# Heads of four attention branches turned by VectorE blocks and GpSimd transfers instead of TensorE

## Chip, cores and metric

One NeuronCore of a Trainium2 chip runs the whole program. The metric is device time in microseconds, the median of several executions.

## What is computed

One layer of a decoder trunk on 256 tokens of width 4096: a normalisation, one projection into all the queries, keys and values of four parallel token mixers, the mixers, a gated merge with an output projection, and a retrieval feed-forward block. What matters here are the scores of the mixers, each a product of a query head with a key head of 128 features:

```python
def qk(t, n, gi):
    return apply_rope(rmsnorm(heads(t, n), qk_gain[gi]), cos, sin)
o_a = stick_breaking_attention(heads(a_q, 4), heads(a_k, 4), heads(a_v, 4))
o_b = dsa_attention(qk(b_q, 4, 0), qk(b_k, 1, 1), ...)
o_c = nsa_attention(qk(c_q, 4, 2), ..., qk(c_ks, 1, 4), ..., qk(c_kw, 1, 5), ...)
o_d = dilated_attention(qk(d_q, 6, 6), qk(d_k, 2, 7), ...)
# in each: s = einsum('bthd,bshd->bhts', q, k) * scale
```

The output has float32 precision. The large products are therefore made three times, on a high and a low part of each operand.

## The kernel before

The program is one stream of 704 slots. A slot is one 512 KB piece of weights (256 rows by 512 columns): SyncE loads it into one of four buffers `w_raw`, ScalarE copies it rounded into `w_hi` (`hi`, line 1207), VectorE forms the rest `w_lo` (`lo`, line 1616), and TensorE runs twelve products of 128x512 on it (`products`, lines 676, 679 and 683; `branch_products`, lines 724, 726 and 730). A conversion may run up to three slots ahead of TensorE, since `hi` of slot s waits for the products of slot s-4 (`chunk_used`). Everything else is put between the slots by hand: on each engine a function `between(s)` issues, after the slot's main work, what tables give for slot s. No scheduler moves anything, and each engine runs its list in order. So an operation of VectorE in slot s is issued some two to three slots ahead of TensorE's slot s.

Slots 0 to 175 are the input projection, in 11 groups of 16 slots. Each group is copied from the accumulators to `proj` (tokens on the partitions) by `evacuate_in` (line 1232), three slots after its end. `norm_piece` normalises and ropes the heads of b, c and d on VectorE, in eight pieces per branch, and raises `heads_ready`. Slots 176 to 287 are the merge stage: per block of 512 output columns one slot of gate products (its result goes through `gates` on ScalarE) and one or two slots of branch products, whose result `merge` on VectorE multiplies with the gate (line 1861), which empties the accumulator bank for the next block.

The scores need queries and keys with the features on the partitions. `turn(n)` (line 780) does this with TensorE: it transposes two heads for both halves of the tokens, four transposes of 128x128, into a bank of `side`, and ScalarE copies the bank to `feat` (`copy_turned`, line 1241) three slots later. The table `TURNS` gives slot, bank, branch and heads. The passes of the softmax branches start in the slots of `PASS_AT`: `scores` (line 854) in that slot, `mask_scores` on VectorE 3 slots later, `exponentials` on ScalarE 4, `turn_probs` on TensorE (line 865) 5, `normalise` on VectorE (lines 1786 to 1800) 6, `weigh_values` on TensorE 7. Pass 6 is the last but one of branch c. The stick-breaking branch a has its scores on line 899, in slots 189 and 205.

The merged rows are already turned later in the program without TensorE: `block_mix` (line 1883) transposes 32x32 blocks with VectorE, `mix_store` and `mix_load` on SyncE's queue write them to DRAM and read them back with the features on the partitions.

Of the kernel before, what the change touches and what calls it, by code (L numbers as in the profile page):

```python
# [28 lines left out]
P = 128  # L29
# [105 lines left out]
def source(s):  # L135

    pair = unrolled_pair(s)
    if pair is None:
# [38 lines left out]
PASS_AT = (75, 82, 110, 117, 124, 131, 138, 145, 157, 165)  # L177
# [56 lines left out]
def build(nc, io):  # L234
# [12 lines left out]
    def const(name, shape, dt=F32):  # L247
# [15 lines left out]
    feat = {"c": at("feat_c", [P, 6, S], F32, MG0), "b": at("feat_b", [P, 7, S], F32, MG0 + 8 * KB),  # L263
            "d": at("feat_d", [P, 8, S], F32, MG0 + 8 * KB), "a": at("feat_a", [P, 8, S], F32, XT0),
            "i": at("idx_t", [P, 3, S], F32, MG0 + 16 * KB)}
# [33 lines left out]
    cmp_zero = at("cmp_zero", [P, P], BF16, cursor[0] + 2 * 32 * 3 * NCMP * 2)  # L299
    dil = const("dil", [P, NT, 3, S])  # L300
# [137 lines left out]
    turned, turned_copied = sems("turned", "turned_copied")  # L438
    z_turned, z_hi_done, z_lo_done = sems("z_turned", "z_hi_done", "z_lo_done")
# [65 lines left out]
    def tile_rows(h):  # L505
        return slice(h * P, (h + 1) * P)

# [60 lines left out]
    with nc.Block() as block:  # L568
# [98 lines left out]
        def _(pe):  # L667
# [84 lines left out]
            def turn(n):  # L752

                s, b, br, blocks = TURNS[n]
                if br == "i":
                    pe.wait_ge(ident_loaded, 32)
                    evacuated(pe, 2)
                elif br == "a":
                    evacuated(pe, NG1 - 1)
                    pe.wait_ge(probs_copied, len(PASSES))  # L760
                    pe.wait_ge(out_lo_done, 6)
                else:
                    pe.wait_ge(heads_ready, "bcd".index(br) * NT + NT)
# [3 lines left out]
                if br == "c":  # L767
                    pe.wait_ge(cmp_ready, 1)
                    pe.wait_ge(out_lo_done, 2)
                for i, blk in enumerate(blocks):  # L770
                    for h in range(NT):
# [4 lines left out]
                        elif br == "i":  # L776
                            c, w = B_IQ + P * blk, P
                        else:
                            c, w = OUT_COL[br] + blk * HD if (br, blk) != ("b", 6) else B_VC, HD
# [3 lines left out]
            def turn_z():  # L783
                last = max(n for n, t in enumerate(TURNS) if t[0] < Z_TURN)
                pe.wait_ge(turned_copied, last + 1)
# [6 lines left out]
            def index_scores(h):  # L792
# [3 lines left out]
                q, nk = feat["i"], (h + 1) * P  # L796
# [6 lines left out]
            def cmp_hidden_part(q):  # L803

                if q == 0:
                    pe.wait_ge(zero_ready, 1)
                    pe.wait_ge(cmp_blocks, 1)
                    pe.wait_ge(turned_copied, 7)
# [25 lines left out]
            def scores(i):  # L834
# [5 lines left out]
                need = {"b": 7, "c": 10, "d": 14}[br]  # L840
                pe.wait_ge(turned_copied, need)
                f = feat[br]
                if br == "b":
                    pairs = [(r, f[:, 4, :]) for r in range(4)]
                elif br == "c":
                    pe.wait_ge(cmp_ready, 1)
                    key = (kt_cmp[:], f[:, 4, :], f[:, 5, :])[part]
                    pairs = [(r, key) for r in range(4)]
                else:
                    pe.wait_ge(z_lo_done, 1)  # L850
                    pairs = [(2 * g + s, f[:, 6 + s, :]) for s in range(2) for g in range(3)]
# [17 lines left out]
            def weigh_values(i):  # L869
                br, h, part = PASSES[i]  # L870
                pe.wait_ge(probs_copied, i + 1)
                if first_part(br, part):
# [3 lines left out]
                    if br == "c":  # L876
                        pe.wait_ge(turned_copied, 10)
# [15 lines left out]
            def stick_z_scores(u):  # L893
                pe.wait_ge(turned_copied, len(TURNS))
                if u:
                    pe.wait_ge(stick_arg, 1)
                for r in range(2):
# [1677 lines left out]
```

## Time and profile before

| | |
|---|---|
| median of 3 runs | 1907.03 us (1906.21 to 1907.64) |
| profiled execution | 1906.17 us |
| its span in the profile | 1904.1 us |
| granted TensorE clock | 1.000 of full |
| busy, TensorE / its weight loads | 1899.7 us / 1566.8 us |
| busy, VectorE / ScalarE / GpSimd | 1463.1 us / 986.2 us / 36.3 us |
| mean DMA traffic | 217 GB/s |

The profile is of one execution; its device time is 2.1 us longer than the span from the first to the last instruction. Times of the rows are microseconds from the span's start unless marked ns. A busy time on TensorE holds overlapping matmuls, so its rows are read by their starts.

### The profile page before, as it was taken

The page shows a single profiled execution, that of the slowest core. Times are in us where ns is not written, and L with a number is a line of the kernel's source. Part 1 is how long each engine was busy: PE and PEld are TensorE (multiplying, and loading weights), DVE is VectorE, ACT ScalarE, POOL GpSimd, SP SyncE. Part 2 cuts the span into 40 slices and gives each one's busy share as a digit, 9 for nine tenths or more (in the row PEclk, how much of TensorE's full clock was granted, in tenths as well). Part 3 has the DMA queues.
Part 4 walks back from the last instruction along what each step waited for, and adds up shares of the span by engine and source line. Part 5 has one row for each costly group of instructions (what it writes and reads, how often), then busy time and mean ns, then how long its engine had stood idle before and what let it go on. Part 6 is the DMA issues. An engine that isn't in the chain of part 4 may idle for free.

```text
span 1904.1 us, 25847 instructions
## 1 busy us (share of the span) xinstructions
PE 1899.7 (100%) x8941; PEld 1566.8 (82%) x8941; DVE 1463.1 (77%) x2139; ACT 986.2 (52%) x1214; POOL 36.3 (2%) x49
## 2 busy tenths in 40 slices
PE   9999999999999999999999999999999999999999
PEld 8888888888888888888888888888887788888887
DVE  6578775585556889989765555899988878999897
ACT  6654644444456655556454464444444455555553
POOL 0010010000000000000000000000000000000000
PEclk9999999999999999999999999999999999999999
DMA  9976667655655668877787776767766678666664
GB/s 321 353 223 166 167 177 202 172 157 157 190 178 175 186 189 289 271 235 233 258 252 239 216 226 218 233 209 214 222 204 194 198 205 290 222 215 222 217 221 155
DMA packets 198833, 412.69 MB, mean 217 GB/s; under 512 B 45793, under 2 KB 124257, under 8 KB 198081
## 3 DMA queue, kind: packets, MB, share of 16 engines
q1 hardware_dynamic: 174048, 369.35, 63.3%
q10 hardware_dynamic: 20976, 25.19, 3.9%
q0 software_dynamic: 3696, 16.65, 2.5%
q8 instruction: 71, 1.16, 0.2%
q14 instruction: 42, 0.34, 0.1%
HBM read 390.15 MB, written 20.97 MB: 216 GB/s over the span
## 4 chain that ended last, share of the span: by engine, by line
PE 99%; DMA 0%; SPq 0%; ACT 0%; DVE 0%; issue 0%
PE acc L676 25%; PE acc L679 25%; PE acc L683 25%; PE acc L724 3%; PE acc L726 3%; PE acc L730 3%; PE acc L1160 2%; PE side L1038 1%; PE side L1040 1%; PE side L1039 1%; PE acc L1166 1%; PE acc L1080 1%; PE acc L1085 1%; PE acc L1079 1%; PE side L854 1%; PE side L966 1%
## 5 line engine op out<-in xcount | busy, mean ns | idle before, releaser
L1616 DVE TENSOR_TENSOR w_lo<-w_raw,w_hi 128x1024 fp32r<-128x1024 f32 (+1 forms) x649 | 784.8, 1213 | 386.7 <-ACT w_hi L1207 381.9
L1207 ACT ACTIVATE w_hi<-w_raw 128x1024 fp32r<-128x1024 f32 (+1 forms) x649 | 681.0, 1052 | 690.6 <-PE acc L683 572.2
L676 PE MATMUL acc<-w_hi,xt_hi 128*128 128x512 f32 x1348 | 365.6, 393 | 0.0
L679 PE MATMUL acc<-w_hi,xt_lo 128*128 128x512 f32 x1348 | 360.7, 389 | 0.0
L683 PE MATMUL acc<-w_lo,xt_hi 128*128 128x512 f32 x1348 | 360.5, 389 | 0.0
L679 PEld LDWEIGHTS acc<-w_hi,xt_lo 128*128 128x128 f32 x1348 | 253.0, 188 | 53.3
L683 PEld LDWEIGHTS acc<-w_lo,xt_hi 128*128 128x128 f32 x1348 | 253.1, 188 | 53.0
L676 PEld LDWEIGHTS acc<-w_hi,xt_hi 128*128 128x128 f32 x1348 | 250.1, 188 | 51.5 <-issue 1.8
L676 PE MATMUL acc<-w_hi,x_hi 128*128 128x512 f32 x640 | 175.1, 395 | 0.0
L679 PE MATMUL acc<-w_hi,x_lo 128*128 128x512 f32 x640 | 171.5, 390 | 0.0
L683 PE MATMUL acc<-w_lo,x_hi 128*128 128x512 f32 x640 | 171.4, 390 | 0.0
L679 PEld LDWEIGHTS acc<-w_hi,x_lo 128*128 128x128 f32 x640 | 120.1, 188 | 25.7
L683 PEld LDWEIGHTS acc<-w_lo,x_hi 128*128 128x128 f32 x640 | 120.1, 188 | 25.6
L676 PEld LDWEIGHTS acc<-w_hi,x_hi 128*128 128x128 f32 x640 | 117.2, 188 | 22.2
L1560 ACT ACTIVATE t_hi<-t_raw 128x1024 fp32r<-128x1024 f32 x46 | 47.7, 1058 | 24.6 <-PE acc L1040 14.9
L2285 DVE TENSOR_TENSOR t_lo<-t_raw,t_hi 128x1024 fp32r<-128x1024 f32 x46 | 54.1, 1218 | 0.0
L1349 ACT ACTIVATE gate<-acc 128x512 f32<-128x512 f32 x64 | 34.8, 596 | 37.3 <-PE acc L683 37.3
L676 PE MATMUL acc<-w_hi,zt_hi 128*128 128x512 f32 x128 | 34.5, 391 | 0.0
L683 PE MATMUL acc<-w_lo,zt_hi 128*128 128x512 f32 x128 | 34.2, 389 | 0.0
L679 PE MATMUL acc<-w_hi,zt_lo 128*128 128x512 f32 x128 | 34.2, 389 | 0.0
L2271 DVE TENSOR_TENSOR t_raw<-w_raw 128x1024 f32<-128x1024 f32 x23 | 28.1, 1221 | 3.9 <-DMA w_raw<-in_stream 3.5
L1861 DVE TENSOR_TENSOR gate<-acc,gate 128x512 f32<-128x512 f32 x48 | 30.7, 681 | 0.0
(376 smaller groups left out, 2050.2 us busy)
## 6 DMA issues: line engine op xcount, KB each, us to landing
w_raw<-in_stream SPq DMA_DIRECT2D x504, 512.0 KB, 4.2
w_raw<-in_w_in SPq DMA_DIRECT2D x16, 496.0 KB, 4.0
w_raw<-in_w_in SPq DMA_DIRECT2D x16, 480.0 KB, 4.1
w_raw<-in_w_in SPq DMA_DIRECT2D x16, 464.0 KB, 3.8
w_raw<-in_w_in SPq DMA_DIRECT2D x16, 448.0 KB, 3.9
w_raw<-in_w_in SPq DMA_DIRECT2D x16, 432.0 KB, 3.8
w_raw<-in_w_in SPq DMA_DIRECT2D x16, 416.0 KB, 4.1
w_raw<-in_w_in SPq DMA_DIRECT2D x16, 400.0 KB, 3.8
```

Of the source, the lines that this page charges most:

```text
L676: pe.matmul(o[h], lhs(k0 + j, h)[0], wh[j], start=first and j == 0, stop=False)
L679: pe.matmul(o[h], lhs(k0 + j, h)[1], wh[j], start=False, stop=False)
L683: mm = pe.matmul(o[h], lhs(k0 + j, h)[0], wl[j], start=False, stop=last and j == 1)
L724: pe.matmul(o, lhs(k0 + j, h)[0], wh[j], start=first and j == 0, stop=False)
L726: pe.matmul(o, lhs(k0 + j, h)[1], wh[j], start=False, stop=False)
L730: mm = pe.matmul(o, lhs(k0 + j, h)[0], wl[j], start=False, stop=last and j == 1)
L1160: pe.matmul(o, xt(2 * kp + j, h)[p], w[0][j], start=kp == 1 and h == 1 and p == 0 and j == 0, stop=False)
L1207: nc.scalar.activation(w_hi[:, slot, 0:width], w_raw[:, slot, 0:width], ACT.Copy).then_inc(hi_ready, 1)
L1349: e = nc.scalar.activation(gate[:, n % 2, h, :], acc[:, 1, h, :], ACT.Sigmoid)
L1560: nc.scalar.activation(flat(hi_tile[:, d]), flat(raw[:, d]), ACT.Copy).then_inc(t_hi_done, 1)
L1616: nc.vector.tensor_tensor(w_lo[:, slot, 0:width], w_raw[:, slot, 0:width], w_hi[:, slot, 0:width].bitcast(F32), ALU.subtract).then_inc(lo_ ...
L2285: nc.vector.tensor_tensor(flat(lo_tile[:, d]), flat(raw[:, d]), flat(hi_tile[:, d]).bitcast(F32), ALU.subtract).then_inc(t_lo_done, 1)
```

## The change

The transposes on TensorE of b's heads 0 to 4 and of all heads of c, d and a go, with ScalarE's copies behind them. In their place, for each branch of the new table `BLOCKED` (slot, heads, parts):

- ScalarE copies the heads in slot s from `proj` into `head_rows`, ordered for the blocks (`copy_heads`);
- VectorE transposes 32x32 blocks in slot s+1 (`block_heads`, one instruction per part) into `head_blk`, with the token as the outer index and (head, half) as the inner one;
- GpSimd writes the four groups of 32 partitions to DRAM in four transfers per part and loads them back in one (`move_heads`).

The tiles `feat` are now [feature, token, head, half]. The score matmuls on TensorE read them directly through `head_tokens` and `head_all`, so from one token to the next they step over all heads and both halves of the tile: 40 B in b (5 heads), 48 B in c (6), 32 B in d (2 tiles of 4) and 64 B in a (8). The passes of c and d start four and three slots later. Blocks 5 and 6 of b and the index heads are still turned by TensorE.

```diff
 TURNS = [(52, 0, "i", (0,)), (53, 1, "i", (1,)), (54, 2, "i", (2,)),
-         (61, 2, "b", (5, 6)), (62, 3, "b", (0, 1)), (64, 2, "b", (2, 3)), (65, 3, "b", (4,)),
-         (104, 3, "c", (0, 1)), (106, 2, "c", (2, 3)), (107, 3, "c", (4, 5)),
-         (144, 2, "d", (0, 1)), (146, 2, "d", (2, 3)), (148, 2, "d", (4, 5)), (150, 2, "d", (6, 7)),
-         (182, 0, "a", (0, 1)), (183, 1, "a", (2, 3)), (184, 2, "a", (4, 5)), (185, 3, "a", (6, 7))]
+         (61, 2, "b", (5, 6))]
+BLOCKED = {"b": (60, 5, 1), "c": (107, 6, 1), "d": (147, 8, 2), "a": (180, 8, 1)}
...
-PASS_AT = (75, 82, 110, 117, 124, 131, 138, 145, 157, 165)
+PASS_AT = (75, 82, 114, 121, 128, 135, 142, 149, 160, 168)
...
+        feat[b] = [at(f"feat_{b}{i}", [P, P, heads // parts, NT], F32, to + i * heads // parts * KB) for i in range(parts)]
+        head_rows[b] = at("head_rows_" + b, [P, parts, 4, heads // parts, NT, 32], F32, to)
...
+    def head_tokens(br, q, h):
+        return head_all(br, q, h, h + 1)[:, 0]
+    def head_all(br, q, h0=0, h1=NT):
+        n = BLOCKED[br][1] // BLOCKED[br][2]
+        return feat[br][q // n][:, :, q % n, h0:h1].rearrange("p t h -> p h t")
...
             def scores(i):
...
-                pe.wait_ge(turned_copied, need)
-                f = feat[br]
+                pe.wait_ge(head_moved, heads_moved(br))
...
-                    mm = pe.matmul(side[:, r // 2, (r % 2) * S:(r % 2) * S + nk], f[:, q, tile_rows(h)],
-                                   key[:, 0:nk], start=True, stop=True)
+                    keys = kt_cmp[:] if key is None else head_all(br, key, 0, h + 1)
+                    mm = pe.matmul(side[:, r // 2, (r % 2) * S:(r % 2) * S + nk], head_tokens(br, q, h),
+                                   keys, start=True, stop=True)
...
             def evacuate_in(g):
+                if g == 9:
+                    act.wait_ge(head_stored, 64 * head_parts("d"))
...
+            def copy_heads(br):
+                _, heads, parts = BLOCKED[br]
+                n = heads // parts
+                if br == "a":
+                    evacuated(act, NG1 - 1)
+                    act.wait_ge(chunk_used, CH_MIX)
+                else:
+                    act.wait_ge(heads_ready, "bcd".index(br) * NT + NT)
...
+                for i in range(parts):
+                    for h in range(NT):
+                        c0 = OUT_COL[br] + i * n * HD
+                        e = nc.scalar.activation(head_rows[br][:, i, :, :, h, :].rearrange("p b k j -> p k b j"),
+                                                 proj[:, h, c0:c0 + n * HD].rearrange("p (k b j) -> p k b j", b=4, j=32),
+                                                 ACT.Copy)
+                    e.then_inc(head_copied, 1)
...
+            def block_heads(br):
+                parts = BLOCKED[br][2]
+                for i in range(parts):
+                    dve.wait_ge(head_copied, head_parts(br) - parts + i + 1)
+                    if br == "c":
+                        dve.wait_ge(scores_ready, 2)
+                    nc.vector.transpose(head_blk[br][i][:].rearrange("p b (t x) -> p b x t", t=32),
+                                        head_rows[br][:, i].rearrange("p b k h j -> p b (k h) j"))\
+                        .then_inc(head_blocked, 1)
...
+            def move_heads(br):
+                parts = BLOCKED[br][2]
+                if head_parts(br) > parts:
+                    pool.wait_ge(head_moved, heads_moved(br) - 16 * parts)
+                for i in range(parts):
+                    pool.wait_ge(head_blocked, head_parts(br) - parts + i + 1)
+                    for a in range(4):
+                        pool.dma_start(head_d[br][:, :, a, i].rearrange("b j x -> j b x"),
+                                       head_blk[br][i][32 * a:32 * a + 32]).then_inc(head_stored, 16)
+                pool.wait_ge(head_stored, 64 * head_parts(br))
+                for i in range(parts):
+                    pool.dma_start(feat[br][i][:].rearrange("p (a t) k h -> p a (t k h)", a=4),
+                                   head_d[br][:, :, :, i].rearrange("b j a x -> (b j) a x")).then_inc(head_moved, 16)
...
             branch_rstd("b")
+            move_heads("b")
             branch_rstd("c")
...
+            move_heads("c")
             branch_rstd("d")
+            move_heads("d")
...
             pool.dma_start(tri[:], io["tri"]).then_inc(stick_loaded, 16)
+            move_heads("a")
```

VectorE's list around pass 6 of branch c, before the change, from the mask of that pass (slot 141) to its normalising multiply (slot 144); `proj` and `rope_tmp` are d's heads being roped, `probs` the probabilities:

```order
L1769 SCALAR_TENSOR_TENSOR probs_62<-side,causal 128x1024
L1772 TENSOR_REDUCE small<-probs_62 128x4
L1774 TENSOR_SCALAR small<-small 128x4
L1616 TENSOR_TENSOR w_lo<-w_raw,w_hi 128x1024
L1661 TENSOR_TENSOR proj<-proj,rope 128x1024
L1662 TENSOR_TENSOR proj<-proj,rope_tmp 128x1024
L1616 TENSOR_TENSOR w_lo<-w_raw,w_hi 128x1024 x2
L1656 TENSOR_TENSOR rope_tmp<-proj,rope 128x8x64
L1657 TENSOR_TENSOR rope_tmp<-proj,rope 128x8x64
L1786 TENSOR_SCALAR small<-small 128x4
L1787 RECIPROCAL small<-small 128x4
L1791 TENSOR_TENSOR small<-small 128x4
```

The same pass in the changed kernel, slots 145 to 148, where the rope pieces are the last of branch d:

```order
L1829 SCALAR_TENSOR_TENSOR probs_68<-side,causal 128x1024
L1832 TENSOR_REDUCE small<-probs_68 128x4
L1834 TENSOR_SCALAR small<-small 128x4
L1663 TENSOR_TENSOR w_lo<-w_raw,w_hi 128x1024
L1708 TENSOR_TENSOR proj<-proj,rope 128x1024
L1709 TENSOR_TENSOR proj<-proj,rope_tmp 128x1024
L1663 TENSOR_TENSOR w_lo<-w_raw,w_hi 128x1024 x2
L1745 STREAM_TRANSPOSE head_blk_d_100<-head_rows_d 128x4x8x32
L1745 STREAM_TRANSPOSE head_blk_d_101<-head_rows_d 128x4x8x32
L1846 TENSOR_SCALAR small<-small 128x4
L1847 RECIPROCAL small<-small 128x4
L1851 TENSOR_TENSOR small<-small 128x4
```

Two block transposes stand ahead of the normalisation, where two rope operations of half a piece stood.

VectorE's list at the start of the merge stage before the change, from the end of branch d's output to the first merges (the first `rows<-acc,gate` belongs to slot 181):

```order
L1807 TENSOR_TENSOR ot_d_lo<-side,ot_d_hi 128x256
L1616 TENSOR_TENSOR w_lo<-w_raw,w_hi 128x1024 x5
L1861 TENSOR_TENSOR rows<-acc,gate 128x512 x2
L1616 TENSOR_TENSOR w_lo<-w_raw,w_hi 128x1024 x3
L1861 TENSOR_TENSOR rows<-acc,gate 128x512 x2
```

And in the changed kernel:

```order
L1867 TENSOR_TENSOR ot_d_lo<-side,ot_d_hi 128x256
L1663 TENSOR_TENSOR w_lo<-w_raw,w_hi 128x1024 x2
L1745 STREAM_TRANSPOSE head_blk_a<-head_rows_a 128x4x16x32
L1921 TENSOR_TENSOR rows<-acc,gate 128x512 x2
L1663 TENSOR_TENSOR w_lo<-w_raw,w_hi 128x1024 x3
```

The transpose of branch a stands directly ahead of the first merge, and d's last output is three slots nearer to it.

## Rows read from the trace of the kernel before

**Rows 1.** The page: busy times, and the chain that ended last by engine
```profile
PE 1899.7 (100%) x8941; PEld 1566.8 (82%) x8941; DVE 1463.1 (77%) x2139; ACT 986.2 (52%) x1214; POOL 36.3 (2%) x49
...
PE 99%; DMA 0%; SPq 0%; ACT 0%; DVE 0%; issue 0%
```

**Rows 2.** TensorE's timeline around one turn: start, length, engine, line, operation, count
```profile
434.80 1.08 PE L683 MATMUL acc<-w_lo,xt_hi 128*128 128x512 f32 x4
435.71 0.60 PE L780 MATMUL side<-ident,proj 128*128 128x128 f32 x4
...
437.07 1.08 PE L679 MATMUL acc<-w_hi,xt_lo 128*128 128x512 f32 x4
437.99 1.07 PE L683 MATMUL acc<-w_lo,xt_hi 128*128 128x512 f32 x4
...
439.80 1.07 PE L679 MATMUL acc<-w_hi,xt_lo 128*128 128x512 f32 x4
```

**Rows 3.** Line 780: count, shortest, median and longest ns, first and last start
```profile
L780 PE MATMUL side<-ident,proj x64: 270/272/273, 137.1 to 547.4; 128*128 128x128 f32 x62, 128*64 128x128 f32 x2
```

**Rows 4.** ScalarE's groups from 100 to 720 us: count, busy us, mean ns, idle before
```profile
L1207 ACT ACTIVATE w_hi<-w_raw 128x1024 fp32r<-128x1024 f32 x207 | 218.2, 1058 | 156.0 <-PE acc L683 122.5 <-PE acc L730 31.2 <-DMA w_raw<-in_w_in 1.8
...
L1277 ACT ACTIVATE cmp_pc<-cmp_in 128x512 bf16<-128x512 f32 x13 | 8.0, 617 | 3.3 <-DVE cmp_in L1714 3.3
```

**Rows 5.** VectorE's groups from 100 to 720 us
```profile
L1696 DVE TENSOR_TENSOR cmp_b<-feat_b,pe_t 128x240 f32<-128x240 f32 x4 | 2.0, 576 | 0.0
...
L1675 DVE TENSOR_TENSOR idx_sum<-idx_sum,idx_tmp 128x256 f32<-128x256 f32 x3 | 1.3, 425 | 0.1
...
L1883 DVE STREAM_TRANSPOSE mix_blk<-mix_rows 128x1024 f32<-128x1024 f32 x1 | 1.2, 1239 | 0.0
```

**Rows 6.** Timeline of all engines from 403 to 419.5 us, pass 6
```profile
404.14 1.22 DVE L1769 SCALAR_TENSOR_TENSOR probs<-side,causal 128x1024 f32<-128x1024 f32 x1 [2.46 <-PE side L854]
...
408.84 2.00 ACT L1207 ACTIVATE w_hi<-w_raw 128x1024 fp32r<-128x1024 f32 x2
...
410.38 2.36 DVE L1616 TENSOR_TENSOR w_lo<-w_raw,w_hi 128x1024 fp32r<-128x1024 f32 x2
...
414.59 1.23 DVE L1800 TENSOR_TENSOR probs<-probs,small 128x1024 f32<-128x1024 f32 x1
...
417.59 1.04 PE L865 MATMUL side<-ident,probs 128*128 128x128 f32 x8
```

**Rows 7.** Timeline from 518 to 534 us, start of the merge stage
```profile
519.62 1.25 ACT L1232 ACTIVATE proj<-acc,small 128x512 f32<-128x512 f32 x2
...
523.15 2.05 ACT L1207 ACTIVATE w_hi<-w_raw 128x1024 fp32r<-128x1024 f32 x2
...
526.52 1.28 DVE L1861 TENSOR_TENSOR rows<-acc,gate 128x512 f32<-128x512 f32 x2
...
529.32 0.62 PE L724 MATMUL acc<-w_hi,ot_b_hi 128*128 128x512 f32 x2
```

**Rows 8.** DMA issues (KB each, median us to landing), and GpSimd's first transfers in its timeline
```profile
mix_blocks<-mix_blk SPq DMA_DIRECT2D x32, 128.0 KB, 4.5
mix_t<-mix_blocks SPq DMA_DIRECT2D x8, 512.0 KB, 6.0
...
518.87 1.34 POOL L2456 DMA_DIRECT2D strict<-in_strict  x2 [137.05 <-PE acc L683]
```

**Rows 9.** TensorE's timeline around d's second score pass, six matmuls of 256 columns
```profile
486.23 1.07 PE L683 MATMUL acc<-w_lo,xt_hi 128*128 128x512 f32 x4
487.14 2.75 PE L854 MATMUL side<-feat_d 128*128 128x256 f32 x12
...
490.66 1.08 PE L679 MATMUL acc<-w_hi,xt_lo 128*128 128x512 f32 x4
```

More of the change, by code:

```diff
@@ L299, in build @@
     cmp_zero = at("cmp_zero", [P, P], BF16, cursor[0] + 2 * 32 * 3 * NCMP * 2)
+    head_blk = {"b": [at("head_blk_b", [P, 4, 5 * 64], F32, cursor[0])],
+                "c": [at("head_blk_c", [P, 4, 6 * 64], F32, MG0 + 8 * KB)],
+                "d": [at(f"head_blk_d{i}", [P, 4, 4 * 64], F32, PJ0 + i * row + in_cols(9).start * 4) for i in range(2)],
+                "a": [at("head_blk_a", [P, 4, 8 * 64], F32, XT0 + 40 * KB)]}
+    head_d = {b: nc.dram_tensor("head_blocks_" + b, (4, 32, 4, parts, heads // parts * 64), F32, kind="Internal").ap()
+              for b, (_, heads, parts) in BLOCKED.items()}
     dil = const("dil", [P, NT, 3, S])
@@ L506, in tile_rows, with heads_moved, head_parts @@
         return slice(h * P, (h + 1) * P)
+    def heads_moved(br):
+        return 16 * head_parts(br)
+    def head_parts(br):
+        return sum(BLOCKED[b][2] for b in list(BLOCKED)[:list(BLOCKED).index(br) + 1])
+    def head_tokens(br, q, h):
[3 more added lines that the diff above has]
+        return feat[br][q // n][:, :, q % n, h0:h1].rearrange("p t h -> p h t")
     def flat(ap):
@@ L757, in turn @@
                     evacuated(pe, 2)
[L758 to L761, printed above, removed]
                 else:
-                    pe.wait_ge(heads_ready, "bcd".index(br) * NT + NT)
+                    pe.wait_ge(heads_ready, NT)
                 before = [m for m in range(n) if TURNS[m][1] == b]
@@ L783, in turn_z @@
             def turn_z():
-                last = max(n for n, t in enumerate(TURNS) if t[0] < Z_TURN)
-                pe.wait_ge(turned_copied, last + 1)
+                pe.wait_ge(cmp_ready, 1)
+                evacuated(pe, (Z_COL + 2 * P - FIRST - 1) // 512 + 1)
                 for h in range(NT):
@@ L1240, in copy_turned @@
                     act.wait_ge(cmp_split, 8)
[L1241 removed]
+                first = blocks[0] - (5 if br == "b" else 0)
+                nc.scalar.activation(flat(whole[br][:, first:first + len(blocks), :]), side[:, b, 0:len(blocks) * S],
                                      ACT.Copy).then_inc(turned_copied, 1)
+            def copy_heads(br):
[4 more added lines that the diff above has]
+                    act.wait_ge(chunk_used, CH_MIX)
+                else:
+                    act.wait_ge(heads_ready, "bcd".index(br) * NT + NT)
+                if br == "b":
+                    act.wait_ge(cmp_split, 8)
+                if br == "c":
+                    act.wait_ge(cmp_ready, 1)
+                if br == "d":
+                    act.wait_ge(head_moved, heads_moved("c"))
+                for i in range(parts):
[5 more added lines that the diff above has]
+                    e.then_inc(head_copied, 1)
             def z_hi():
@@ L1485, in between @@
                         copy_turned(n)
+                for br, (at_slot, _, _) in BLOCKED.items():
+                    if s == at_slot:
+                        copy_heads(br)
                 if s == Z_TURN + LEAD:
```

43 lines of the change are left out of this document (23 added, 20 removed).

## Prediction

> **What bounds the kernel now.** I read the page first: TensorE is busy for the whole span and 99% of the chain that ended last is its own, so the time is the length of TensorE's instruction stream [rows 1]. Anything taken out of that stream is gained one for one, and anything that makes TensorE wait is lost one for one. Then the timeline of TensorE around one removed turn. From the start of the last four products of a slot (434.80) to the start of the second four of the next slot (437.07) pass 2.27 us with a turn between; one slot later the same stretch takes 1.81 us (437.99 to 439.80). A turn of four transposes so costs 0.46 us, 0.115 us each [rows 2]. The matmul durations of 272 ns [rows 3] overlap and must not be added up. Last, the timelines of VectorE and ScalarE where the change queues new work, to see how much room is left before TensorE needs what stands behind it.
>
> The sum is made against the profiled execution, 1906.2 us (span 1904.1), which is 0.9 us under the median of the runs, 1907.0; the result is then given against the median. About 0.2% (3.8 us) is what a measurement of this kernel can tell from no change.
>
> **Removed from TensorE.** Of 66 transposes on line 780 (64 are in the trace [rows 3]) the change keeps twelve, those of the index heads and of blocks 5 and 6 of b. Gone are 10 of b, 12 of c, 16 of d and 16 of a: 54 x 0.115 = **-6.2 us**, all of it on the path. The 14 ScalarE copies out of PSUM that followed them go too; in their place come ten copies from SBUF of 512 to 1024 columns, 0.62 us per 512 and 1.06 us per 1024 [rows 4]. That is about as much time as before, on an engine that is half idle: nothing by itself.
>
> **Added to VectorE.** Five block transposes: 1280, 1536, 2 x 1024 and 2048 columns. The one that the trace shows, 1024 columns into a packed tile, took 1.24 us [rows 5], which is 1.04 ns a column after 0.16 us of start. The new ones write each column 32 to 64 B from the last. No row shows such a write. The nearest row is a strided read: line 1696 takes its input 64 B apart, 240 columns in 576 ns, where 256 packed ones take 425 ns [rows 5]. After the same start that is 1.74 ns a column. So 2048 columns take between 2.3 and 3.7 us, 1024 between 1.24 and 1.94. VectorE has room in general; two places matter.
>
> *Slot 147/148, branch d.* In pass 6 TensorE turns probabilities five slots after the scores, and VectorE must have normalised them. Before, the scores ended at about 404.1, the normalising multiply started at 414.59 and was over 1.9 us before TensorE's turn at 417.59 [rows 6]. The pass moves by four slots, so I lay the same times over it. VectorE's last rope piece ends as its next w_lo starts, at 410.38. ScalarE is through its exponentials and one conversion at 409.84; in the same slot it empties group 8 (two copies, 1.25 us as for the last group [rows 7]: 411.1), then come the four new copies (some 0.55 us from start to start, a little under the row's 0.62: 413.3), and only then the next w_hi (414.3). VectorE's w_lo behind it ends at 415.5, the two block transposes take 2.3 to 3.9 us, and the three small operations (0.62 us) and the multiply (1.14 us) stand behind them: 419.6 to 421.1. TensorE waits **2.0 to 3.5 us**.
>
> *Slot 180/181, branch a.* In the merge stage TensorE's first product of slot 180 (529.32 before) needs the bank that VectorE's merge of block 0 empties. Before, that merge began at 526.52 [rows 7]. Now ScalarE, free at 523.15, does a w_hi (524.2), the two copies of 1024 (526.3) and the next w_hi (527.3); VectorE's w_lo ends at 528.5, the transpose of 2048 columns at 530.8 to 532.2, and the first half of the merge at 531.4 to 532.9. TensorE waits **2.1 to 3.6 us**.
>
> I take the middle of both, 2.8 + 2.8 = **+5.6 us**, since the write is like the packed row in kind and like the strided row in its steps. At b (slot 60/61) VectorE's queue has no TensorE consumer within five slots, and at c (107/108) no pass is open: nothing there.
>
> **Added to GpSimd.** Per part four stores and one load. The same pattern on other queues took 4.5 us to land for a store and 6.0 us for a load, and GpSimd issued two transfers in 1.34 us [rows 8]: 4 x 0.67 + 4.5 + 0.67 + 6.0 = 14 us. The tightest consumer is c, blocked in slot 108 and needed in slot 114: six slots of 2.72 us and the lead of some two that VectorE has, 21 us. a has eight slots, d twelve, b fourteen. Hidden, with 7 us to spare at the tightest. If that is used up, TensorE waits for the rest.
>
> **Moved into TensorE's operands.** The features now lie with the token outermost, so 60 score matmuls read query and key in steps of 40 B (b), 48 B (c), 32 B (d) and 64 B (a). The moving columns are 1536, 3072, 2304 and 1536, together 8448. Packed, six matmuls of 256 columns lengthened the same stretch from 1.81 to 4.43 us [rows 9], so 1.71 ns a column, in two passes of 0.85 ns. No row shows TensorE reading with such a step. Lower bound: nothing, if its port does not care. Upper bound: each read takes the 1.74 ns that VectorE needed [rows 5], twice a column, +1.77 ns x 8448 = 15.0 us. That row has the 64 B step of branch a; I take it whole for a (2.7 us) and half for the smaller steps of the others (6912 x 0.89 = 6.1 us): **+8.8 us**.
>
> The page "Advanced Engine Details and Errata" of the Trainium skill, section "SBUF Cachelines", speaks against this layout: SBUF is read in lines of 16 bytes, and full speed wants at least two hits on a line. It gives no price; by it every one of the four steps would pay in full, and the sum would end near 1923. VectorE's row at 64 B agrees with it; for TensorE nothing here shows it.
>
> **Sum.** -6.2 + 5.6 + 8.8 = +8.2 us: 1914.4 for the profiled execution, **1915 us** against the median.
>
> **Rivals.**
>
> 1. *The strides are free to TensorE.* For it: TensorE takes an fp32 column in 0.85 ns a pass and the products' columns in half of that, so it may fetch well ahead. Against it: the one strided row of the trace. Then only the two waits are left, -6.2 + 4.1 to 7.1, that is 1905 to 1908: no change.
> 2. *Strides free and the waits absorbed* (the other side). The waits rest on 2 to 3.5 us past the need at two places; if ScalarE's copies run before heads_ready costs anything, or TensorE's sequencer finds bank and probabilities in time, the removed transposes stand alone: 1907.0 - 6.2 = 1901. It decides where VectorE's transposes end over 2 us earlier than I lay them out. For it: before the change TensorE waited nowhere. It becomes faster by over 0.2% as soon as waits and strides cost together less than 2.4 us.
> 3. *Every strided read pays in full*, with the slow writes: -6.2 + 7.1 + 15.0 = +15.9, 1923.
> 4. *A transfer lands late*, in c first: each 1 us beyond the 7 us of room is 1 us of TensorE. With 5 us late and free strides: 1911.
>
> **How the numbers follow.** My forecast and rival 3 are one mechanism of two sizes: together 0.50 (0.36 and 0.14). Rival 1 has 0.34, rival 2 0.12, rival 4 0.04. Faster 0.12, same 0.36 (rival 1 and the smallest of the forecast's), slower 0.52. The range has to hold rival 1 and nearly all of rival 3 and leaves out rival 2: 1902 to 1924. The forecast's own range is 1911 to 1924.
>
> **What the changed profile would show.** Step 1: line 780's successor with 12 transposes, and 54 fewer matmuls. Step 2: in TensorE's waits one of 2 to 3.5 us for VectorE's probs at the turn of pass 6, and one for VectorE's rows in the first merge; a busy share of TensorE a little under 100%. Step 3: the 12 records of a d pass of 256 columns take clearly more than 2.6 us of the stream, and so do a's; if they take 2.6, rival 1 or 2 holds. Step 4: GpSimd's loads land before slots 75, 114, 160 and 189, with no TensorE wait for a feature tile. The block transposes' mean (1.24 or 1.94 us for 1024 columns) tells which end the waits take. I am wrong if TensorE's scores keep their length, or if it waits for something not named here, a transfer above all.

## The result, and the profile after

| | before | after |
|---|---|---|
| median of 4 runs each, us | 1906.99 (1906.21 to 1907.64) | 1929.04 (1927.91 to 1929.31) |
| ratio, 95% interval | | 1.0115 (1.0097 to 1.0132) |
| profiled execution, us (span) | 1906.2 (1904.1) | 1929.3 (1927.5) |
| mean granted TensorE clock | 1.000 | 0.997 |

The kernel became slower by 22 us. I had forecast 1915, with a range of 1902 to 1924: the sign was right, the size was wrong, and the time lies outside the range. Two single executions of the experiments, one of e5 at 5576 us and one of the kernel before at 7792 us, are left out.

The page of the changed kernel, busy times and chain, against [rows 1]:

```profile
PE 1916.7 (99%) x8887; PEld 1578.6 (82%) x8887; DVE 1475.7 (77%) x2144; ACT 986.3 (51%) x1210; POOL 50.6 (3%) x74
...
PE 98%; ACT 1%; DVE 1%; DMA 0%; issue 0%; SPq 0%; ACTq 0%
```

TensorE has 54 matmuls fewer (8941 to 8887), as counted, and is busy 17 us longer. The chain of the end now passes through ScalarE and VectorE for one per cent each; before it was TensorE's alone. So there are two things to look for: matmuls that take longer, and waits.

**The waits.** TensorE's waits after the change, what it waited for, us in total, times, longest:

```profile
PE side L882 <- DVE probs L1860: 3.3, 1, 3.3
PE acc L750 <- DVE rows L1921: 3.1, 1, 3.1
```

These are the two waits of the prediction, at the two places named. The timeline round the first, pass 6 with d's block transposes in front of its normalisation, which answers to [rows 6]:

```profile
429.57 2.19 ACT L1283 ACTIVATE head_rows_d<-proj 128x512 f32<-128x512 f32 x4
...
433.88 4.00 DVE L1745 STREAM_TRANSPOSE head_blk_d<-head_rows_d 128x1024 f32<-128x1024 f32 x2
...
438.35 1.23 DVE L1860 TENSOR_TENSOR probs<-probs,small 128x1024 f32<-128x1024 f32 x1
...
439.64 1.97 PE L882 MATMUL side<-ident,probs 128*128 128x128 f32 x8 [3.27 <-DVE probs L1860]
...
441.26 1.80 PE L702 MATMUL acc<-w_hi,xt_hi 128*128 128x512 f32 x4
...
442.89 1.08 PE L705 MATMUL acc<-w_hi,xt_lo 128*128 128x512 f32 x4
```

And round the second, a's block transpose in front of the first merge, which answers to [rows 7]:

```profile
540.65 2.01 ACT L1283 ACTIVATE head_rows_a<-proj 128x1024 f32<-128x1024 f32 x2
...
544.77 3.66 DVE L1745 STREAM_TRANSPOSE head_blk_a<-head_rows_a 128x2048 f32<-128x2048 f32 x1
...
548.29 1.25 DVE L1921 TENSOR_TENSOR rows<-acc,gate 128x512 f32<-128x512 f32 x2
...
549.10 1.19 PE L750 MATMUL acc<-w_hi,ot_b_hi 128*128 128x512 f32 x2 [3.11 <-DVE rows L1921]
550.09 1.06 PE L752 MATMUL acc<-w_hi,ot_b_lo 128*128 128x512 f32 x2
```

Read the chain backwards in each: TensorE starts as VectorE's last operation delivers, that operation starts as the transposes end, and those could not start until ScalarE's copies were done and a w_lo had been made. The transposes took 3657 ns for 2048 columns and 2.0 to 2.15 us for 1024, at the slow end of what I had bounded from [rows 5] (3.7 and 1.94 us) or a little beyond it.

**The clock.** In the last two fences something else is odd. Eight transposes take 1.97 us where the same eight took 1.04 [rows 6], and two products of the merge 1.19 and 1.06 where they took 0.62 [rows 7]. The busy times by stretch of 2 us (PE, PEld, DVE, ACT, POOL, then the granted TensorE clock, DMA share and GB/s) show why:

```profile
438.00:440.00 2.00, 0.36 (x2) 0.37 (x3) 1.93 (x4) 0.00 (x0) 2.00 (x5) 0.80 0.86 213
440.00:442.00 2.00, 2.00 (x10) 1.90 (x9) 1.85 (x2) 0.36 (x1) 1.05 (x2) 0.50 0.81 240
...
549.00:551.00 2.00, 1.90 (x5) 1.56 (x6) 1.85 (x3) 0.00 (x0) 1.98 (x4) 0.50 0.46 100
...
553.00:555.00 2.00, 2.00 (x6) 1.55 (x5) 0.00 (x0) 0.35 (x1) 0.00 (x0) 0.50 1.01 260
555.00:557.00 2.00, 2.00 (x9) 1.60 (x9) 1.25 (x2) 0.71 (x1) 0.54 (x1) 0.94 1.00 365
```

The number behind POOL's is the granted clock: 0.50 is the lower of the two levels, 1.2 GHz against 2.4. TensorE stood still ahead of both stretches, and came back at half speed. At the first place it got its full clock back after some 3 us, at the second after 6. The prediction had no term for this.

**The score matmuls.** TensorE's timeline round d's second score pass, six matmuls of 256 columns in two passes of fp32 each, which answers to [rows 9]:

```profile
507.82 1.08 PE L709 MATMUL acc<-w_lo,xt_hi 128*128 128x512 f32 x4
508.73 2.01 PE L871 MATMUL side<-feat_d,feat_d 128*128 128x256 f32 x4
...
513.84 1.52 PE L702 MATMUL acc<-w_hi,xt_hi 128*128 128x512 f32 x4
515.20 1.08 PE L705 MATMUL acc<-w_hi,xt_lo 128*128 128x512 f32 x4
```

From 507.82 to 515.20 pass 7.38 us; the same stretch took 4.43. The weight loads grew too. Load times of two tiles, least, median and longest ns:

```profile
L871 PEld LDWEIGHTS side<-feat_c x32: 341/343/373, 325.5 to 421.7; 128*128 128x128 f32 x32
...
L871 PEld LDWEIGHTS side<-feat_d x8: 312/324/337, 484.1 to 513.3; 128*128 128x128 f32 x8
```

against this one before the change:

```profile
L854 PEld LDWEIGHTS side<-feat_c x32: 186/190/192, 314.3 to 403.5; 128*128 128x128 f32 x32
```

Measured like this (from the start of the last product ahead of a pass to the start of the second group of products behind it), the twelve score passes take:

| pass (step in the change) | before | after | e1, both packed | e2, weights strided | e3, moving strided |
|---|---|---|---|---|---|
| b, 128 and 256 columns (40 B) | 2.72, 4.42 | 3.73, 6.33 | 2.72, 4.41 | 3.56, 4.50 | 3.66, 6.31 |
| c, 128 twice (48 B) | 2.72, 3.58 | 3.95, 4.77 | 2.72, 3.59 | 3.86, 4.68 | 3.64, 4.50 |
| c, 15 twice (queries 48 B, keys packed) | 3.58, 4.44 | 4.68, 5.54 | 3.58, 4.44 | 4.67, 5.54 | 3.59, 4.45 |
| c, 256 twice (48 B) | 4.81, 5.28 | 6.80, 7.15 | 4.80, 5.28 | 5.32, 5.64 | 6.64, 7.13 |
| d, 128 and 256 (32 B) | 3.17, 4.43 | 4.67, 7.38 | 3.16, 4.43 | 4.57, 4.68 | 4.62, 7.37 |
| a, 256 twice (64 B) | 2.23, 2.70 | 3.51, 3.99 | 2.23, 2.69 | 2.58, 3.03 | 3.51, 3.97 |
| sum | 44.1 | 62.5 | 44.1 | 52.6 | 59.4 |

(The last three columns belong to the experiments below.) The passes account for 62.5 - 44.1 = 18.4 us. The transposes' -6.2, the waits' 3.27 + 3.11 = 6.4 and what the stretches behind the waits lost besides close the span's +23.4 us. That last part: 435.30 to 442.89 is 7.59 us, where a run without the wait (e11 below) has 2.72, so 4.87 are lost, 1.6 more than the wait; in the merge stage the same comparison gives 12.63 against 6.35, that is 6.28, 3.2 more than the wait. The sum is -6.2 + 18.4 + 6.4 + 4.8 = 23.4. Its first term is the forecast's; e5 below measures -6.5.

**GpSimd's transfers** (KB each, median us from issue to landing) against [rows 8]:

```profile
head_blocks_c<-head_blk_c POOLq DMA_DIRECT2D x4, 192.0 KB, 4.2
feat_c<-head_blocks_c POOLq DMA_DIRECT2D x1, 768.0 KB, 7.9
```

c's stores were issued from 304.62, its load at 312.44, so it landed at 320.3, and TensorE's first pass on it began at 325.77. No TensorE wait names a feature tile. The transfers are hidden, as forecast, though with less room: from the first store to the landing pass 15.7 us where I had 14, and 5.4 us were left where I had 7.

### The profile page after: what moved, and what is told of

The parts are those of the page before. It is cut to its first block, busy times and chain, and to the rows that moved or that the text cites. A ratio compares the mean times of both kernels' runs of the same rounds, so it can differ in the third digit from the quotient of the medians.

```text
span 1927.5 us, 25751 instructions
## 1 busy us (share of the span) xinstructions
PE 1916.7 (99%) x8887; PEld 1578.6 (82%) x8887; DVE 1475.7 (77%) x2144; ACT 986.3 (51%) x1210; POOL 50.6 (3%) x74
## 4 chain that ended last, share of the span: by engine, by line
PE 98%; ACT 1%; DVE 1%; DMA 0%; issue 0%; SPq 0%; ACTq 0%
PE acc L702 25%; PE acc L705 25%; PE acc L709 25%; PE acc L750 3%; PE acc L752 3%; PE acc L756 3%; PE acc L1178 2%; PE side L871 2%; PE side L1056 1%; PE side L1057 1%; PE side L1058 1%; PE acc L1184 1%; PE acc L1098 1%; PE acc L1097 1%; PE acc L1103 1%; PE side L984 1%
## 5 line engine op out<-in xcount | busy, mean ns | idle before, releaser
L1335 ACT ACTIVATE probs<-probs,small 128x128 f32<-128x128 f32 (+2 forms) x44 | 18.3, 417 | 39.0 <-DVE small L1834 39.0
```

## The experiments

Twelve kernels ran, four to ten executions each; the kernel before, run beside each of them on the same chip, had medians of 1906.0 to 1906.8 us. The theory after the result: the removed transposes gain 6 us, the strided operands cost 18, the two waits 6.4, and the clock behind them some 4 more. The rivals: that the strides cost less and something else in the new route slows TensorE (GpSimd's transfers or VectorE's transposes beside it), and that the fall of the clock has a cause of its own.

### e1, e2, e3: which operand pays

Both operands, or one of them, are read with step 1 from the same tiles; nothing else changes. Here `packed` takes as many columns as are needed from the head's own stretch of 256 in the flattened tile. They are not the head's columns, so the scores of e1, e2, e3 and e5 are not the right ones; the amount of work is the same.

```diff
-                    keys = kt_cmp[:] if key is None else head_all(br, key, 0, h + 1)
-                    mm = pe.matmul(..., head_tokens(br, q, h), keys, ...)
+                    keys = kt_cmp[:] if key is None else packed(br, key, (h + 1) * P)
+                    mm = pe.matmul(..., packed(br, q, P), keys, ...)
```

e1 has both lines and the same two in a's scores, e2 the keys' alone, e3 the queries' alone.

> The changed kernel, but the score matmuls read both operands from the same feature tiles with a step of one element; the scores are then of the wrong columns. Everything else stays: copies, block transposes, transfers, slots. Theory 1 (the steps cost TensorE's reads): the stretches around the twelve groups of score matmuls fall back to their lengths of before, 18.4 us in sum, so 1910 to 1911 us; both waits of 3.1 to 3.3 us and the low clock behind them stay. Rival (the stretches are longer for another reason, such as tiles that a transfer has just written, or GpSimd's traffic): no change, 1929 us.

> As the changed kernel, but only the moving operand (the keys; in a the queries) is read with a step of one; the weights are still read with their steps, and the scores are of wrong columns. A pass of 15 columns took 0.24 us with strided weights, so the strided weight load itself takes that long. If a pass takes the longer of its load and its columns, the 128-column passes stay at 0.24 us and only the 44 passes of 256 columns get shorter, from 0.455 to 0.24 us: 9.5 us less, 1919 to 1920 us. If load and columns add up, the gain is 8448 columns x 2 x 0.94 ns = 15.9 us: 1913 us. If only the moving side pays (rival), all 18.4 us: 1911 us.

> The mirror: weights read with a step of one, the moving operand with its steps, scores of wrong columns. If a pass takes the longer of load and columns, only the 16 passes of 15 columns and the 128-column passes of branch c gain, some 2.2 + 0.5 us: 1926 us. If load and columns add up, or the weight loads are what pays (rival), it falls by more than 5 us, to below 1924 us.

Measured: e1 1908.63 us (1906.35 to 1910.54), e2 1916.41 (1914.68 to 1917.36), e3 1924.81 (1924.46 to 1925.25). The table above has their passes. In e1 every pass is back at its length of before to 0.01 us, with the new engines' work and the transfers still running beside it: only the steps lengthened the passes. In e2 the weights alone make 8.5 us of it, in e3 the moving operand alone 15.3, together 18.4 and not their sum, 23.8. In each pass it is about the longer of the two that counts: the greater of e2 and e3, added up over the twelve, is 17.9. Where 256 columns move, the moving operand sets the length; where 15 move, the weights do; at 128 both are about equal. Weight loads run beside the matmul before them, and a late one shows only where the matmul is short.

In its passes e2 gave back 62.5 - 52.6 = 9.9 us, the 9.5 of its first expectation (the longer of load and columns): beside 256 columns the slow weight loads are mostly hidden (0.1 to 0.5 us a pass). Its time came out 3 us under that expectation's 1919 to 1920. In its profiled run the stretches round the two waits are shorter than in the changed kernel as well, 6.90 us against 7.59 and 11.32 against 12.63, though the waits are as long (3.28 and 3.08): 2.0 us less time lost to the clock. e3 is the same case: 3.1 us from the passes where 2.7 were expected, and 1.4 from the two stretches (7.52 and 11.33), which makes 1924.5 of the changed kernel's 1929.0.

e1 came out 2 us under its expectation in the median and on it in the profiled run (1910.41). Its waits were still 3.26 and 3.11. Every execution has its mean granted clock on record, and e1's ten fall into groups by it: two at 1906.4 and 1906.5 us with 1.000, four at 1908.0 to 1908.7 with 0.998 to 0.999, four at 1910.3 to 1910.5 with 0.997 to 0.998. The fastest are e5's time (below) and the 6.4 us of waits, to about 1 us. So two waits of over 3 us together cost some 4 us more than themselves in some executions of one kernel and next to nothing in others.

### e4, e5: the waits, and the removed transposes alone

```diff
-BLOCKED = {..., "d": (147, 8, 2), "a": (180, 8, 1)}
+BLOCKED = {..., "d": (149, 8, 2), "a": (181, 8, 1)}
```

e4 is the changed kernel with these slots; e5 is e1 with them.

> The changed kernel with two numbers of its table changed: d is copied in slot 149 instead of 147, a in slot 181 instead of 180, so that no block transpose stands ahead of a normalisation or merge that TensorE needs at once. Theory 2 (two waits of 3.3 and 3.1 us, each followed by a stretch at the lower clock, 1.6 and 3.1 us more): all 11.1 us go, 1918 us, no wait above 0.5 us and a granted clock of 1.000. Rival (the clock falls for another reason, such as the longer score matmuls): only the 6.4 us of waiting go, 1922 to 1923 us, and the clock stays below 1. Second rival: the feature tiles land too late, and TensorE waits for them in slot 160 or 189.

> All of the score matmuls' operands of b, c, d and a are read with step 1 (wrong columns of the tile, so the output is wrong) and the block transposes stand one slot later for a (slot 181) and two later for d (149). Neither the strided reads nor the two waits are left, so only the removed transposes remain: 1907.0 - 6.2 = 1900.8 us. If the clock's fall behind the waits had a cause of its own, or if the later slots cost anything, it ends at 1902 to 1906. A rival by which the transposes were hidden all along gives 1907.

Measured: e4 1918.48 us (1917.43 to 1920.69), e5 1899.55 (1899.38 to 1899.64), ratio to before 0.9966 (0.9952 to 0.998). Of e4's waits only one of 1.3 us at the start of the kernel is left, which every kernel here has. e5 has neither strides nor waits and gains 6.5 us: the 54 transposes were worth what I took for them, and VectorE's new work and GpSimd's transfers cost TensorE nothing. From e5 the losses stack up. Against the kernel before that ran beside each, e5 stands at -6.5 us, e11 (below) at +12.4 and the changed kernel at +22.1: the strides add 18.9 us, the waits and the clock 9.7.

### e6: one wait alone

Only d's slot is 149; a's stays at 180.

> The changed kernel with d's block transposes at slot 149 instead of 147, a's left where it is. It takes away the wait of 3.27 us for the probabilities of pass 6, and, if the lower clock follows from that wait, its 1.6 us too: 1929.0 - 4.9 = 1924.1 us, with the granted clock at 1.00 from 438 to 444 and still about 0.5 behind the wait in the merge stage. If the clock's falls are not tied to the waits, only 3.3 us go: 1925.8.

Measured: 1924.24 us (1923.90 to 1924.89), 4.8 under the changed kernel, where the wait itself was 3.27. The clock at d, from 434 to 442 us, is 1.00, and the stretch takes 2.72 us, so the clock's part there belongs to d's wait. In the merge stage the wait is 3.12 and the stretch that took 12.63 us takes 11.37: the clock came back sooner. The two stretches give 4.9 + 1.3 us; a fall at another place (last section) takes 0.75 back, and the profiled runs differ by 5.4.

```profile
545.00:547.00 2.00, 2.00 (x7) 1.56 (x8) 1.85 (x3) 0.00 (x0) 2.00 (x4) 0.75 0.59 125
547.00:549.00 2.00, 2.00 (x6) 1.57 (x5) 0.82 (x1) 0.00 (x0) 0.00 (x0) 0.50 0.84 217
549.00:551.00 2.00, 2.00 (x9) 1.60 (x9) 0.44 (x1) 1.06 (x1) 0.00 (x0) 0.90 0.99 248
```

The same wait of 3.1 us so cost 3.2 us more than itself in one execution and 1.9 in another.

### e7, e9, e10: the steps by themselves, in the kernel before

All the transposes stay with TensorE, at their slots; only the layout of the feature tiles changes, and with it ScalarE's copies write and the score matmuls read with a step. e7 has the steps of the change; e10 keeps heads in pairs (16 B), e9 each head for itself with its two tiles of tokens interleaved (8 B).

```diff
-    feat = {"c": at("feat_c", [P, 6, S], F32, MG0), ...
-            "d": at("feat_d", [P, 8, S], F32, MG0 + 8 * KB), ...
+    feat = {"c": at("feat_c", [P, 1, P, 6, NT], F32, MG0), ...
+            "d": at("feat_d", [P, 2, P, 4, NT], F32, MG0 + 8 * KB), ...
...
+    def head_all(br, q, h0=0, h1=NT):
+        n = feat[br].shape[3]
+        return feat[br][:, q // n, :, q % n, h0:h1].rearrange("p t h -> p h t")
```

For e10 the tiles are [P, heads/2, P, 2, NT], for e9 [P, heads, P, 1, NT].

> The kernel before with all its 66 transposes by TensorE and all its slots; only the tiles of the transposed heads are laid out as in the change (token outermost, steps of 40, 48, 32 and 64 B), so ScalarE's copies write them and the score matmuls read them with these steps. If the strided operands cost TensorE 18.4 us by themselves: 1907.0 + 18.4 = 1925.4 us. If part of what I put down to them came from something else in the change (GpSimd's transfers, VectorE's transposes beside them): under 1920. If ScalarE's strided writes take so long that a copy comes late: over 1926, with a TensorE wait for side.

> The kernel before with its transposes by TensorE, each head's tile for itself with the two tiles of tokens interleaved: score matmuls read queries and keys in steps of 8 B, two columns to 16 bytes. With 40 to 64 B the same control took 1925.4. The Trainium skill, page Advanced Engine Details and Errata, section SBUF Cachelines, has full speed from two hits on a line of 16 bytes: by that this step is free, 1907 us, and the six matmuls of 256 columns in d's second pass take 4.43 us of the stream as before. If any step above 4 B costs the same: 1925.4, and 7.38 us. If the price grows with the step, something between.

> The same control with heads in pairs, so steps of 16 B. By the same section of the skill one column to a line of 16 bytes pays in full: 1925.4 us, d's second pass 7.38 us, no less than at 32 to 64 B. If the price grows with the step (my prediction took half of it below 64 B), 16 B costs less than 40 B: 1912 to 1922.

Measured: e7 1925.43 us (1925.11 to 1926.19), e9 1906.88 (1906.38 to 1908.59; ratio 1.0002, 0.9993 to 1.0012), e10 1925.28 (1923.66 to 1925.74). All three times are on their expectation. e7's passes are those of the changed kernel to 0.01 us each and sum to the same 62.5. Its page shows a clock of 1.000, and there is no wait at either of the change's two places: the strides alone cost 19.2 us of span (1904.1 to 1923.3). 18.4 of them are the passes. The rest goes with two small waits, 0.7 us for `out_t_lo` at a place without strided operands, which the kernel before has not, and 1.0 us for `w_hi` in the first 10 us, where it has 0.5; why they appear stays open. d's second pass with a step of 8 B (e9):

```profile
486.73 1.07 PE L691 MATMUL acc<-w_lo,xt_hi 128*128 128x512 f32 x4
487.64 2.88 PE L861 MATMUL side<-feat_d 128*128 128x256 f32 x12
...
491.29 1.07 PE L687 MATMUL acc<-w_hi,xt_lo 128*128 128x512 f32 x4
```

and with a step of 16 B (e10):

```profile
498.01 1.07 PE L691 MATMUL acc<-w_lo,xt_hi 128*128 128x512 f32 x4
498.92 5.64 PE L861 MATMUL side<-feat_d 128*128 128x256 f32 x12
...
505.34 1.07 PE L687 MATMUL acc<-w_hi,xt_lo 128*128 128x512 f32 x4
```

4.56 us at 8 B, 7.33 at 16 B, 7.38 at 32 B. Between 8 and 16 B stands a cliff, and behind it next to no slope: the twelve passes sum to 44.9 us at 8 B (packed 44.1), 61.8 at 16 B and 62.5 with the steps of the change. The section "SBUF Cachelines" of the Trainium skill's page "Advanced Engine Details and Errata" asks for two hits on a line of 16 bytes for full speed, which a step of 8 B gives and one of 16 B does not; the cliff agrees, and here are its prices. The weight loads' medians are 190 to 192 ns packed, 194 to 196 at 8 B, 310 to 329 at 16 B and, in the changed kernel, 293 (a, 64 B) to 370 (c's passes of 15, 48 B).

### e11, e12: shorter waits

e11 is the changed kernel with slots 148 and 181.

> The changed kernel with d's block transposes at slot 148 (147 in the change) and a's at 181 (180): against the run with slots 149 and 181, 1918.5 us, only a wait of 3.27 - 2.72 = 0.5 us for the probabilities of pass 6 is left. If a wait of this length lowers the clock as the 3.3 us did: 1918.5 + 0.5 + 1.6 = 1920.6. If the clock stays at 1.00 behind it: 1919.0.

Measured: 1918.86 us (1918.14 to 1919.29), clock 1.000. There is no wait at either place, so the question was not put: I had taken the wait to shrink by the length of a slot, but in slot 148 the normalisation stands ahead of the block transposes in VectorE's list and is not held up at all.

```profile
432.37 1.23 DVE L1860 TENSOR_TENSOR probs<-probs,small 128x1024 f32<-128x1024 f32 x1
433.65 1.23 DVE L1663 TENSOR_TENSOR w_lo<-w_raw,w_hi 128x1024 fp32r<-128x1024 f32 x1
434.80 4.17 DVE L1745 STREAM_TRANSPOSE head_blk_d<-head_rows_d 128x1024 f32<-128x1024 f32 x2
```

It is the clean reference, though: strides, no waits, full clock.

e12 is e8 (below) with the change's slots 147 and 180.

> The version whose loads pack the features (1899.15 us with slots 149 and 181), with the change's own slots 147 and 180. VectorE's block transposes write packed: two of d in 2.4 us instead of 4.0, the one of a in 2.3 instead of 3.7. So the waits shrink to 3.27 - 1.6 = 1.7 us (probabilities of pass 6) and 3.11 - 1.35 = 1.75 us (first merge), and without a fall of the clock: 1899.2 + 1.7 + 1.75 = 1902.6. If waits of 1.7 us lower the clock for as long as those of over 3 us did (1.6 and 3.05 us more): 1907.3. If GpSimd's loads of a, which would start no earlier, come late: more than that, with a wait for feat_a.

Measured: 1904.16 us (1902.77 to 1906.55), ratio 0.9986 (0.9977 to 0.9996), between the two expectations. The waits are 1.65 and 1.81. Granted clock behind the first, and behind the second:

```profile
427.00:429.00 2.00, 1.09 (x9) 1.09 (x10) 2.00 (x3) 0.00 (x0) 2.00 (x5) 1.00 0.94 329
429.00:431.00 2.00, 2.00 (x11) 1.62 (x10) 1.13 (x1) 1.96 (x3) 1.03 (x2) 1.00 0.88 277
...
529.00:531.00 2.00, 1.90 (x6) 1.57 (x7) 1.85 (x3) 0.35 (x1) 1.85 (x4) 0.74 0.54 133
531.00:533.00 2.00, 2.00 (x6) 1.55 (x5) 1.06 (x1) 0.00 (x0) 0.34 (x1) 0.50 0.87 217
533.00:535.00 2.00, 2.00 (x9) 1.62 (x9) 0.13 (x1) 1.06 (x1) 0.00 (x0) 0.90 1.01 250
```

Behind 1.65 us the clock stayed, and the stretch lost only 0.2 us besides the wait (4.58 against 2.72). Behind 1.81 us it fell, and the stretch lost 1.9 besides (10.03 against 6.35). Its ten runs spread over 3.8 us, and by the mean granted clock of each they order like e1's: seven with 1.000 lie at 1902.8 to 1904.9 us, three with 0.999 at 1904.8 to 1906.6. The profiled one is the slowest, and it also waits 1.4 us for `w_hi` in its first 10 us, where the changed kernel waits 0.5. Where in the unprofiled executions the clock fell is not on record.

### e8: a version that beats both

The features can come out packed if the load puts every run of 32 tokens in its place. VectorE then writes packed as well.

```diff
-    feat[b] = [at(..., [P, P, heads // parts, NT], F32, ...
+    feat[b] = [at(..., [P, heads // parts, NT, P], F32, ...
...
-                    nc.vector.transpose(head_blk[br][i][:].rearrange("p b (t x) -> p b x t", t=32),
+                    nc.vector.transpose(head_blk[br][i][:].rearrange("p b (x t) -> p b x t", t=32),
...
-                    pool.dma_start(feat[br][i][:].rearrange("p (a t) k h -> p a (t k h)", a=4),
-                                   head_d[br][:, :, :, i].rearrange("b j a x -> (b j) a x"))...
+                    for a in range(4):
+                        pool.dma_start(feat[br][i][:, :, :, 32 * a:32 * a + 32].rearrange("p k h t -> p (k h) t"),
+                                       head_d[br][:, :, a, i].rearrange("b j (x t) -> (b j) x t", t=32))...
```

> A whole version that could beat both: VectorE's block transposes write packed runs of 32 tokens, and GpSimd's loads, four per part, put each run of 128 B in its place, so that the features lie packed as before the change; slots 149 and 181. TensorE's operands are packed: if the loads land in time, 1901 us, with VectorE's transpose of 2048 columns at 2.3 us instead of 3.7. The loads move the same bytes in pieces of 128 B instead of 1 to 2 KB; they took 4.5 to 7.9 us. c is the tightest, with some 7 us to spare by the timeline of the changed kernel: if its loads take over 15 us TensorE waits for them and loses clock behind it, which gives 1905 to 1925 with a wait for feat_c at pass 2.

Measured: 1899.15 us (1898.85 to 1900.61), ratio to before 0.9966 (0.9952 to 0.998). It gains 0.34% on the kernel before and 30 us on the changed one, and matches e5, which only read as if packed. Its block transposes and its transfers of c:

```profile
L1745 DVE STREAM_TRANSPOSE head_blk_d<-head_rows_d x2: 1203/1221/1239, 425.4 to 426.6; 128x1024 f32<-128x1024 f32 x2
...
L1745 DVE STREAM_TRANSPOSE head_blk_a<-head_rows_a x1: 2305/2305/2305, 524.4 to 524.4; 128x2048 f32<-128x2048 f32 x1
```

```profile
head_blocks_c<-head_blk_c POOLq DMA_DIRECT2D x4, 192.0 KB, 4.4
feat_c<-head_blocks_c POOLq DMA_DIRECT2D x4, 192.0 KB, 5.3
```

The transpose of 2048 columns takes 2.3 us instead of 3.7, and 1024 take 1.22, as the packed row in [rows 5] has them. GpSimd issues c's four loads in 4.08 us from 308.36; the last lands near 317, and TensorE's first pass on it begins at 322.26. Pieces of 128 B instead of 1.5 KB lengthened c's load from 7.9 us to some 8.5, inside the room there was.

## Why the prediction was wrong, step by step

- **Removed transposes, -6.2.** Right: e5 has -6.5. Reading the price from two stretches of the stream and not from the 272 ns of a record [rows 2, 3] was what made it so. No record was missing: 64 of the 66 transposes stand on line 780 and two on line 774.
- **The two waits, +5.6.** Right in place, mechanism and size: 3.27 and 3.11, both in the ranges I gave (2.0 to 3.5, 2.1 to 3.6) and near their slow ends, since a strided write by VectorE costs about what its strided read costs (1.7 to 1.9 ns a column against the row's 1.74). I took the middle between the two rows; the row with the step was the right one.
- **Strided operands, +8.8.** This is the first step that failed. "I take it whole for a (2.7 us) and half for the smaller steps of the others": a measured 2.6, the others 15.8 where I had 6.1. There is no "half" at a smaller step; e10 shows full price at 16 B and e9 next to none at 8 B. The rule of the Trainium skill that I quoted against the layout said so, and I gave it 0.14 as part of rival 3. With the measured 18.4 for the 8.8 the sum would have come to 1925.
- **Its upper bound, 15.0.** Also too low. It counted moving columns alone, and for these it was right (e3: 15.3). The weights are strided as well: the two passes of 15 columns, whose keys are packed, cost 2.2 us that no moving column pays for, and at 128 columns load and matmul are about equally slow. With 18.4 in place of 15.0, rival 3 would have come to 1926. (The score matmuls are 52, not 60; the sum goes by their 8448 columns, which are right.)
- **Clock behind the waits, no term.** The second step that failed. A wait of TensorE's was priced at its length; it cost 4.9 and 6.3 us where it lasted 3.3 and 3.1. The page "TensorE: Matmul & The Clock Gate" of the Trainium skill has the clock follow how busy the engine has been, and the trace of the changed kernel agrees (0.50 behind both waits); before the change TensorE waited only in its first 10 us, with the clock at 1.00, so no row showed it. What decides whether it falls, and for how long, stays open.
- **Rivals 1 and 2** (free strides; waits absorbed) fell: e7 shows the strides' price without the change's waits, and both waits were there. **Rival 4** (a late transfer) fell too: no wait for a feature tile in any run, not even with loads in pieces of 128 B.
- **The signs I had named.** The 54 matmuls fewer, the two waits, the lengthened d and a passes and the loads ahead of their slots were all found. "I am wrong if it waits for something not named here": it did not wait, it ran at half speed.

The whole, by the spans of the profiled runs: -6.2, +18.4, +6.4 and, for the clock, +4.8 us, against my -6.2, +8.8, +5.6 and nothing. By the medians it is -6.5, +18.9 and +9.7 (e5, e11 and the changed kernel).

## What to carry to other kernels

If a new route saves TensorE instructions, look first at how the matmuls will read what it delivers: in fp32 a step of 8 B cost next to nothing here (0.8 us over the twelve passes), and steps of 16 to 64 B doubled the time of a moving column (0.85 to about 1.8 ns a pass in d's second pass) and added 54 to 95% to a weight load, so a layout that needs the step must be repaired in the transfer or in the copy that writes it. A wait of a TensorE that is otherwise never idle can cost more than its length, here from nothing to 3.2 us more; move the work that causes it behind its consumer in the queue, here by one slot. And when two rows bound a price, take the one that shares the property in question (here the step), not the middle.

## What was not expected of the hardware

- The price of a step is a cliff between 8 and 16 B (1907 against 1925 us) and nearly flat from 16 to 64 B.
- Weights and moving operand overlap in their slowness: 8.5 and 15.3 us singly, 18.4 together. The Trainium skill's page "TensorE: Matmul & The Clock Gate", section "Step-by-step: what each phase is for", gives weights and moving operand a read port each, and the runs agree.
- Behind a wait of 1.65 us the clock held, behind one of 1.81 us it fell, and behind waits of 3.1 us in the merge stage it was back, counted from the end of the wait, after about 6 us in the changed kernel, 4.5 in e6 and under 3 in e1. So the cost of a wait is itself uncertain by 1 to 3 us, and a range should hold that.

The clock can fall without any wait, too. In e4, and at the same place in e6, TensorE was busy throughout, but behind c's strided pass of 256 columns the granted clock fell (busy times by stretch of e4, the granted clock behind POOL's):

```profile
394.00:396.00 2.00, 2.00 (x6) 1.57 (x5) 0.00 (x0) 0.40 (x1) 0.00 (x0) 0.87 0.76 219
396.00:398.00 2.00, 2.00 (x6) 1.47 (x6) 1.16 (x1) 0.00 (x0) 0.00 (x0) 0.50 0.08 30
398.00:400.00 2.00, 2.00 (x9) 1.59 (x8) 1.93 (x4) 0.44 (x2) 0.00 (x0) 0.78 0.00 0
```

The changed kernel, e7 and e11 passed the same matmuls at 1.00. In e4 and e6 the pass took 7.55 us instead of 6.80. Why the clock falls there in some executions only stays open.
